# A sparse-attention layer's steps taken in twos, with PSUM banks shared between scores and transposes

## What is computed

```
q = rms_norm(h @ w_in[q]);  kslc, vslc, kwin, vwin from h @ w_in        # 16 heads of 64 in 4 groups
p_c = masked_softmax(q @ k_cmp - slope * dist)                           # compressed branch, 31 blocks
p_s = masked_softmax(q @ kslc  - slope * dist)                           # selected branch
p_w = masked_softmax(q @ kwin  - slope * dist)                           # window branch
o = gate0 * p_c @ v_cmp + gate1 * p_s @ vslc + gate2 * p_w @ vwin
x = x + o @ w_out
```

## Time and profile before

| | us |
|---|---|
| median of 3 runs (2063.76 to 2066.28) | 2065.8 |
| the profiled execution | 2062.16 |
| its span, first to last instruction | 2060.4 |
| PE busy | 2023.5 (98%) |
| DVE busy | 1412.0 (69%) |
| ACT busy | 971.4 (47%) |
| POOL busy | 151.7 (7%) |

### The profile page before, as it was taken

The page is one execution under the profiler, slowest core; times in us unless marked ns, Lnnn a source line. Parts: engine busy times, 40 slices in busy tenths (PEclk is TensorE's granted clock), DMA queues, the critical chain, the costliest instruction groups (busy, mean ns, idle before and its releaser), DMA issues. The chain is left out here.

```text
span 2060.4 us, 36832 instructions
## 1 busy us (share of the span) xinstructions
PE 2023.5 (98%) x14803; PEld 1756.5 (85%) x14803; DVE 1412.0 (69%) x2743; ACT 971.4 (47%) x1874; POOL 151.7 (7%) x140
## 2 busy tenths in 40 slices
PE   9999999999999999999999999999999999999997
PEld 9997777899988887789999887888888888788986
DVE  5247874988864767578887556766666667586576
ACT  5337982555500266545553004554444453566554
POOL 1113330000000400000000002000000000120000
PEclk9999999999999999999999999999999999999998
DMA  5240001233332221013332321211111110112211
GB/s 188 83 144 22 2 2 62 93 103 104 103 132 82 94 84 62 21 62 113 103 103 93 123 102 51 103 62 62 61 61 61 61 61 20 74 67 103 80 45 42
DMA packets 30664, 159.35 MB, mean 77 GB/s; under 512 B 3392, under 2 KB 3904, under 8 KB 17856
## 3 DMA queue, kind: packets, MB, share of 16 engines
q1 hardware_dynamic: 30240, 157.24, 21.6%
q10 hardware_dynamic: 288, 0.20, 0.0%
HBM read 155.33 MB, written 2.10 MB: 76 GB/s over the span
## 5 line engine op out<-in xcount | busy, mean ns | idle before, releaser
L231 PE MATMUL ps<-late_parts,panel_upper 128*128 128x256 f32 (+1 forms) x1376 | 458.8, 333 | 0.0
L230 PE MATMUL ps<-late_parts,panel_upper 128*128 128x256 f32 (+1 forms) x1260 | 430.3, 342 | 5.4 <-issue 1.8
L232 PE MATMUL ps<-late_parts,panel_parts 128*128 128x256 f32 (+1 forms) x1260 | 424.4, 337 | 0.0
L221 DVE TENSOR_TENSOR panel_parts<-panel_sb,panel_upper 128x512 fp32r<-128x512 f32 (+1 forms) x330 | 321.1, 999 | 14.3 <-ACT panel_upper L734 8.7
L230 PE MATMUL ps<-panel_upper,hT_parts 128*128 128x256 f32 (+2 forms) x964 | 295.1, 306 | 2.2 <-DVE h_lower L919 1.4
L232 PE MATMUL ps<-panel_upper,h_lower 128*128 128x256 f32 (+2 forms) x964 | 283.4, 294 | 0.0
L231 PE MATMUL ps<-panel_parts,hT_parts 128*128 128x256 f32 (+2 forms) x964 | 282.1, 293 | 0.0
L231 PEld LDWEIGHTS ps<-late_parts,panel_upper 128*128 128x128 f32 x1376 | 258.7, 188 | 25.8
L230 PEld LDWEIGHTS ps<-late_parts,panel_upper 128*128 128x128 f32 x1260 | 236.7, 188 | 36.8 <-issue 4.4
L232 PEld LDWEIGHTS ps<-late_parts,panel_parts 128*128 128x128 f32 x1260 | 237.9, 189 | 28.5
L230 PE MATMUL ps<-hT_parts,panel_upper 128*128 128x512 f32 (+1 forms) x492 | 191.8, 390 | 1.7 <-PEq L4268 1.7
(11 more groups left out here) (544 smaller groups left out, 3757.8 us busy)
## 6 DMA issues: line engine op xcount, KB each, us to landing
panel_sb<-ffn_gate_up_w SPq DMA_DIRECT2D x76, 512.0 KB, 4.4
panel_sb<-gdn_w SPq DMA_DIRECT2D x24, 1024.0 KB, 4.8
panel_sb<-ffn_down_w SPq DMA_DIRECT2D x22, 1024.0 KB, 4.9
panel_sb<-nsa_w SPq DMA_DIRECT2D x13, 1024.0 KB, 4.8
panel_sb<-gla_w SPq DMA_DIRECT2D x12, 1024.0 KB, 4.9
panel_sb<-gdn_out_w SPq DMA_DIRECT2D x8, 1024.0 KB, 4.8
panel_sb<-ffn_gate_up_w SPq DMA_DIRECT2D x6, 1024.0 KB, 5.0
panel_sb<-nsa_out_w SPq DMA_DIRECT2D x4, 1024.0 KB, 4.9
```

Of the source, the lines that this page charges most:

```text
L221: return engine.tensor_tensor(out, src, hi.bitcast(F32), ALU.subtract)
L230: mm(out, w_hi, x_hi, start=start, stop=False, skip_group_check=skip_group_check)
L231: mm(out, w_hi, x_lo, start=False, stop=False, skip_group_check=skip_group_check)
L232: return mm(out, w_lo, x_hi, start=False, stop=stop, skip_group_check=skip_group_check)
```

## The change

From step 6 the steps go in twos (a batch is v and v+1 for even v). PE does `scores(v+2)`, `scores(v+3)`, `turn(v)`, `turn(v+1)`, `values(v-1)`, `values(v)`. ACT does `exps(v+2)`, `turned(v)`, `exps(v+3)`, `turned(v+1)`, and after those a pair's `upper_o` and one `upper_out`. DVE does both weightings, then both `biased`, then `head_bias`, `lower_o` and the previous batch's `lower_out`. Scores and transposes share three pairs of PSUM banks; each takes the pair whose last use was earliest, and waits until that use has been read. There are four `prob` buffers instead of three, `POOL_STEPS` is 4, and the fourth compressed group's work moves one step later. Its `cmp_exp` stands ahead of `exps(7)`, and `exps(7)` ahead of the copy of step 5. The diff shows the banks first, then the loops of PE, ACT and DVE.

```diff
-    NB = 3
+    NB = 4
-    POOL_STEPS = 6
-    OUT_PIECE_AT = (8, 9, 10, 13, 15, 18, 19, 20, 23, 24, 25, 28, 33, 34, 35, 38)
+    POOL_STEPS = 4
+    TWOS_FROM = 6
+    OUT_PIECES = 16
...
+    for two in range(TWOS_FROM, STEPS, 2):
+        SHARED += [(SCORE, v) for v in (two + 2, two + 3) if v < STEPS] + [(TURN, two), (TURN, two + 1)]
...
+            banks = min(last_in, key=lambda b: SHARED.index(last_in[b]))
+        BANKS_OF[use], BANKS_BEFORE[use] = banks, last_in[banks]
...
+    def await_banks(pe, use):
+        kind, v = BANKS_BEFORE[use]
+        if kind == SCORE:
+            pe.wait_ge(S("n_biased"), ops_before(v + 1))
+        else:
+            pe.wait_ge(S("n_pT"), v + 1)
...
-            if v == 3:
+            if v == 4:
                 cmp_scores(3)
-            if v == 5:
+        for v in range(TWOS_FROM, STEPS, 2):
+            if v + 2 < STEPS:
+                scores(v + 2)
+                scores(v + 3)
+            turn(v)
+            if v == TWOS_FROM:
                 turn_pc(3)
+            turn(v + 1)
+            values(v - 1)
+            values(v)
...
+            if v == TWOS_FROM - 1:
+                cmp_exp(3)
+                exps(v + 2)
...
+        for v in range(TWOS_FROM, STEPS, 2):
+            for u in (v, v + 1):
+                if u + 2 < STEPS:
+                    exps(u + 2)
+                turned(u)
+                if u == TWOS_FROM:
+                    save_pc(3)
+            for u in (v, v + 1):
+                if u % PAIR_STEPS == 1:
+                    upper_o(u // PAIR_STEPS - 1)
+            if (v - TWOS_FROM) // 2 < OUT_PIECES:
+                upper_out((v - TWOS_FROM) // 2)
...
+        for v in range(TWOS_FROM, STEPS, 2):
+            for u in (v, v + 1):
+                weighted(u)
+            for u in (v + 2, v + 3):
+                if u < STEPS:
+                    biased(u)
+            for pair, ab in BIAS_IN.get(v, []):
+                head_bias(pair, ab)
+            for u in (v, v + 1):
+                if u % PAIR_STEPS == 2:
+                    lower_o(u // PAIR_STEPS - 1)
+            if v > TWOS_FROM:
+                lower_out((v - TWOS_FROM) // 2 - 1)
```

More of the change, by code:

```diff
@@ L285, in build_in @@
     bias_pair0 = take(T)
-    kcmp_st = take(P)
+    kcmp_st = hidden[:, 0, :]
     kc_sum, q_gain = take(1), take(1)
@@ L396, in pair_step @@
         return pair, pieces
+    TURN, SCORE = "turn", "score"
+    SHARED = [(SCORE, 0), (SCORE, 1), (SCORE, 2), (TURN, 0), (SCORE, 3), (TURN, 1)]
+    for v in range(2, TWOS_FROM):
+        SHARED += [(SCORE, v + 2), (TURN, v)]
+    for two in range(TWOS_FROM, STEPS, 2):
+        SHARED += [(SCORE, v) for v in (two + 2, two + 3) if v < STEPS] + [(TURN, two), (TURN, two + 1)]
+    BANKS_OF, BANKS_BEFORE = {}, {}
+    last_in = {0: None, 2: None, 4: None}
+    for n, use in enumerate(SHARED):
+        kind, v = use
+        if v < TWOS_FROM:
+            banks = 4 if kind == TURN else 2 * (v % 2)
+        else:
+            banks = min(last_in, key=lambda b: SHARED.index(last_in[b]))
+        BANKS_OF[use], BANKS_BEFORE[use] = banks, last_in[banks]
+        last_in[banks] = use
+    def await_banks(pe, use):
+        kind, v = BANKS_BEFORE[use]
+        if kind == SCORE:
+            pe.wait_ge(S("n_biased"), ops_before(v + 1))
+        else:
+            pe.wait_ge(S("n_pT"), v + 1)
     def ops_before(v):
@@ L620, in scores @@
             else:
-                pe.wait_ge(S("n_biased"), ops_before(v - 1))
+                await_banks(pe, (SCORE, v))
             for t, br, at, n in pieces:
@@ L626, in scores @@
                         r = head_rows(ab)
-                        last = mm(ps[:, 2 * (v % 2) + ab, at + c:at + end], qT[r, pair, tok(t)], kT[r, br * GROUPS + pair // 2, c:end], start=True, stop=True)
+                        last = mm(ps[:, BANKS_OF[SCORE, v] + ab, at + c:at + end], qT[r, pair, tok(t)], kT[r, br * GROUPS + pair // 2, c:end], start=True, stop=True)
             last.then_inc(S("n_scores"), 1)
@@ L633, in turn @@
             else:
-                pe.wait_ge(S("n_pT"), v)
+                await_banks(pe, (TURN, v))
             for ab in range(2):
@@ L642, in turn @@
                 for tile in range(TT):
-                    last = nc.tensor.transpose(ps[:, 4 + ab, tok(tile)], prob[v % NB][:, ab, tok(tile)], ident[:])
+                    last = nc.tensor.transpose(ps[:, BANKS_OF[TURN, v] + ab, tok(tile)], prob[v % NB][:, ab, tok(tile)], ident[:])
             last.then_inc(S("n_turned"), 1)
@@ L682, in pe_nsa @@
         turn_queries(N_Q[3], 1)
-        for v in range(1, STEPS):
-            if 1 < v < STEPS - 2:
+        for v in range(1, TWOS_FROM):
+            if v > 1:
                 scores(v + 2)
@@ L874, in turned @@
                 act.wait_ge(S("n_valued"), v - 1)
-            nc.scalar.copy(pT[v % 2][:, :, :], ps[:, 4:6, :]).then_inc(S("n_pT"), 1)
+            nc.scalar.copy(pT[v % 2][:, :, :], ps[:, BANKS_OF[TURN, v]:BANKS_OF[TURN, v] + 2, :]).then_inc(S("n_pT"), 1)
         def upper_out(n):
@@ L894, in act_nsa, with copied @@
         exps(2)
-        for v in range(STEPS):
-            if 2 <= v < STEPS - 1:
+        def copied(v):
+            turned(v)
+            if v % PAIR_STEPS == 1 and v > 1:
+                upper_o(v // PAIR_STEPS - 1)
+        for v in range(TWOS_FROM):
+            if v >= 2:
                 exps(v + 1)
+            if v == TWOS_FROM - 1:
+                cmp_exp(3)
+                exps(v + 2)
             if v == 2:
                 save_pc(2)
-            turned(v)
+            copied(v)
             if v == 0:
                 cmp_exp(2)
[L903 to L910, removed]
+        for v in range(TWOS_FROM, STEPS, 2):
[10 more added lines that the diff above has]
+                upper_out((v - TWOS_FROM) // 2)
         upper_o(NPAIR - 1)
@@ L1117, in biased @@
                 for ab in range(2):
-                    nc.vector.tensor_tensor_reduce(out=prob[v % NB][:, ab, at:at + n], in0=ps[:, 2 * (v % 2) + ab, at:at + n], in1=bias_of(pair)[ab][:, T - n:T],
+                    nc.vector.tensor_tensor_reduce(out=prob[v % NB][:, ab, at:at + n], in0=ps[:, BANKS_OF[SCORE, v] + ab, at:at + n], in1=bias_of(pair)[ab][:, T - n:T],
                                                    scale=1.0, scalar=3e38, op0=ALU.add, op1=ALU.min,
@@ L1162, in dve_nsa @@
         save_queries(N_Q[3], 1)
-        for v in range(1, STEPS):
+        for v in range(1, TWOS_FROM):
             if v >= POOL_STEPS:
                 weighted(v)
-            if v + 2 < STEPS:
-                biased(v + 2)
-            if v + 1 < min(POOL_STEPS, STEPS):
+            biased(v + 2)
+            if v + 1 < POOL_STEPS:
                 inverse_sums(v + 1)
-            if v % PAIR_STEPS == 2 and v > 2:
-                lower_o(v // PAIR_STEPS - 1)
             if v == 1:
                 cmp_weights(2)
-            if v == 3:
+            if v == 4:
                 cmp_bias(3)
-            if v == 4:
+            if v == 5:
                 cmp_weights(3)
[L1178 to L1181, removed]
+            if v < 3:
+                head_bias(1, v - 1)
+        BIAS_IN = {}
+        for pair in range(2, NPAIR):
+            free = TWOS_FROM if pair == 2 else max(u for u in range(TWOS_FROM, STEPS, 2) if u < PAIR_STEPS * (pair - 1))
+            for ab in range(2):
+                BIAS_IN.setdefault(free + 2 * ab if pair > 2 else free, []).append((pair, ab))
+        for v in range(TWOS_FROM, STEPS, 2):
[11 more added lines that the diff above has]
+                lower_out((v - TWOS_FROM) // 2 - 1)
         lower_o(NPAIR - 1)
```

## The result

| | before | after |
|---|---|---|
| median, us | 2063.73 (20 runs, 2060.49 to 2066.28) | 2068.78 (20 runs, 2066.09 to 2071.18) |
| the profiled execution, us | 2062.16 | 2067.06 |
| its span, us | 2060.4 | 2065.2 |
| mean granted clock | 0.996 | 0.994 |

The ratio is 1.0024, with an interval of 1.0018 to 1.0030. The changed kernel is slower by 5.05 us by the medians and 4.9 by the profiled executions; the forecast was +8 for the latter, and 2073.8 us for the median. The direction was right and the size too large. Of the 5.0 us between 2073.8 and 2068.78, 3.1 are the profiled execution's own (2070.2 forecast, 2067.06 measured). The other 1.9 are the step from there to the median: 3.6 was added, from three runs of the kernel before; over 20 runs each it is 1.6 before and 1.7 after.

What follows compares the result with a forecast made beforehand. PE was taken to set the pace, ACT close behind. Start 3.8, batches 18 and 28 4.3, end 3.4, less 4.3 idle, gave +7.2; with 0.8 sharing, 2070.2 us profiled, 2073.8 median, range 2065 to 2079.

Steps and rivals of the forecast that it cites:

- The start: Up to values(8): later cmp_scores(3) and cmp_bias delay VectorE's chain, and values(5) waits for save_pc(3); loss 3.8 us.
- Batches 18 and 28: lower_o waits for upper_o on VectorE, so biased and the second transposes come late; 2.15 us each, together 4.3.
- The end: Batch 38, delayed by batch 36 with no scores to cover: ends near 8.5 instead of 5.1, loss 3.4 us.
- Sharing between VectorE and GpSimd: Back-to-back VectorE weightings beside GpSimd's in five delayed batches: 0 to 2.5 us, about 0.55 a time at most; 0.8 taken.
- No order of the steps changes these: PE's group prices, start to next start, were taken as fixed: transposes 1.03, compressed product 1.05, values 1.02, scores 1.08 us.
- its idle time: PE's idle 4.3 us within the 103.4 from scores(12) to the output projection, which the change was to win.
- VectorE's waits of over 3 us for `upper_o`: Sign that the forecast is right: such a wait where turn(9), turn(19) and turn(29) are late.
- The projection: Sign that the forecast is right: the output projection starts 7 to 10 us later than 308.84.
- The one of no change: Rival: start costs less, half the late stands are covered, 2 x 1.1 in batches 18 and 28; +3.3, 2069; chance 0.17.
- ACT did not become the bound: Slower rival: ACT becomes the bound, each batch from 10 on losing 0.4 to a late copy; 2079, chance 0.10.
- The faster rival: Batches run at PE's pace, VectorE's stand at lower_o short; 4.3 idle goes, 1 to 2 stay; -4.5, 2061; chance 0.11.
- My warning of a granted clock under 1.00: Sign that the forecast is wrong: a granted clock under 1.00 in the loop, adding to all; no size given.

Runs made afterwards that it cites:

- e5: The kernel before with only the start of the change (four prob buffers, POOL_STEPS 4, fourth compressed group one step later): 2067.78 us, ratio 1.0017.
- e7: The changed kernel with unread transposes filling PE's gaps ahead of turn(5) and turn(38): 2069.87 us, ratio 1.0031.
- e1: The changed kernel with lower_o of pairs 0, 2, 4 and 6 on VectorE one batch later: 2058.07 us, ratio to before 0.9973.
- e3: The changed kernel with the edits of e1 and e2 together: 2055.56 us, ratio to before 0.9966.
- e8: The same kernel as e3, profiled a second time, nothing changed: 2054.75 us in one run.
- e4: e3, but PE's scores and transposes alternate again within each batch: 2058.08 us, ratio to before 0.9973.
- e2: The changed kernel with cmp_scores(3) one step earlier and cmp_bias(3) ahead of biased(6): 2067.14 us, ratio to before 1.0017.
- e9: The same kernel as e2, profiled a second time, nothing changed: 2066.27 us in one run.

## Why the prediction was right in sign and wrong in size

**The start, +3.8 forecast, 4.2 measured.** Most steps named came: `turn(5)` at 189.45 with the offset, where my terms end the weighting at 189.3, `biased(8)` at 195.5 for my 194.8, `values(5)` at 199.2 for 198.5, `turn(9)` at 206.75 for 206.2. `turn(7)` came at 197.7 for my 196.3, and not behind `biased(8)`: PE itself was late with its groups at the lower clock, and VectorE had stood still for 1.07 us, for `scores(8)`:

```profile
194.98 0.69 DVE L1164 CUSTOM_DVE_ANT_0 arena_sb<-ps,hT_sb 128x512 f32<-128x512 f32 x1 [1.07 <-issue]
```

By e5 some 3.6 of it come with the start's own edits. Part of the agreement is luck: the clock's fall, worth 1.2 us at `values(5)` by e7, was not in the sum, while pairs of `values` and `scores` at steps 6 to 10 were cheaper than I had them.

**Batches 18 and 28, 2 x 2.15 forecast, 2 x 2.63 measured.** The chain was right to 0.3 us: `turn(19)` starts 5.60 into its batch and I had 5.33. `lower_o(2)` is 0.4 later than I had it (1.20 into the batch for 0.76), and some 0.1 is GpSimd at work beside the second weighting; the rest of the chain was a little shorter than its terms. The gap of PE is in two parts, 1.28 for the weighting and 1.18 for `biased`. The other 0.2 of the difference is that batch 18 without the stall is shorter than I assumed: in e1 it has its second transposes at 2.97 (5.89 less 1.02 and 1.90), not 3.17. A stall counts from where the engine would have been, and PE would have been earlier.

**The end, +3.4 forecast, 4.8 measured.** `turn(38)` starts 3.29 into the batch, for my 3.3. Then 0.8 come from the clock (e7), and GpSimd's three weightings take 2.73 us where I had 1.02 and about 1.2:

```profile
307.00 2.73 POOL L1270 TENSOR_SCALAR arena_sb<-arena_sb 128x512 f32<-128x512 f32 x3 [7.49 <-DVE arena_sb L1172]
```

**Sharing between VectorE and GpSimd, 0.8 forecast.** The second weighting takes 0.90 instead of 0.80 for pieces of 128 and 384 columns (above, and the earlier trace rows), and 1.15 for two of 256 at 192.76 where others in the same trace take 0.90. That is 0.10 to 0.25 a time, 0.7 for five: the value taken was right, and its high end of 0.55 a time is not seen. The exclusive hold that the Trainium skill describes (SBUF — State Buffer, "Who interferes with whom") would have kept VectorE waiting at 238.48 until GpSimd's first weighting, begun at 237.87 and some 1.02 long, had ended. This place shows at most 0.10 of that 0.4; whether this weighting is of the kind that takes the hold, no run shows.

**The step that failed: "No order of the steps changes these".** I took the price of each group from a timeline in which each has a neighbour of another kind, and summed 6.26 us a batch. The order does change them. Two groups of one kind in a row take 1.95, 1.92 and 1.90 us, not 2.16, 2.06 and 2.04. In the stretch from `scores(12)` to the projection of e3 there are 14 such pairs of `scores`, 12 of `turn` and 12 of `values` (the others are parted by a wait or a compressed product): 14 x 0.21 + 12 x 0.14 + 12 x 0.14 = 6.3.

| us | forecast | measured |
|---|---|---|
| before, less its idle time | 103.4 - 4.3 | 103.4 - 4.3 |
| cheaper pairs | 0 | -6.3 |
| idle time left in e3 | 0 | +2.9 |
| stalls behind `lower_o` | +7.7 | +9.8 |
| sum, the sharing apart | 106.8 | 105.5 |

The trace has 105.3. The 9.8 is that less the 95.5 of e1 and e3. The 2.9 I read off e3's timeline: 0.3 at the transposes of batches 14, 16, 24, 26, 34 and 36, 0.1 in six others, and 0.36 at the last `values`. In batches 16, 26 and 36 it is a wait for `biased`. By the first three rows e3 should take 95.7, and takes 95.5. So the change has a gain of some 6 us that I did not see, and its stalls cost 2 us and its small waits 3 us more than I gave them.

The whole then reads: the forecast was 8.0 and the span grew by 4.8 (the execution by 4.9). From step 12 on the loop lost 1.9 and not 3.4 + 0.8, which is 2.3 less; the start lost 0.4 more; 0.5 was ahead from before the change and 0.8 is less behind the loop, both of which I had at nothing. Neither is more than the same code varies by between the traces (`cmp_scores(3)`, where it follows `values(2)`, starts between 179.47 in e8 and 180.95 in e4). 8.0 - 2.3 + 0.4 - 0.5 - 0.8 = 4.8.

**The signs and the rivals.** VectorE's waits of over 3 us for `upper_o` came, and the wait of `values(5)`. The projection came 5.6 us later (6.1 with the offset) and not 7 to 10. None of the rivals held as such. The one of no change had 2069, next to the measured 2068.78, but that is luck: by its mechanism the stands of batches 18 and 28 would have been 1.1 us each, and they are 2.63. ACT did not become the bound: with `lower_o` moved (e1) PE runs at its own pace but for the small waits, with ACT's work unchanged. The faster rival said that without VectorE's stand at `lower_o` the loop would win 4.3 less 1 to 2; e1 takes the stand away, and the loop wins 7.9 (103.4 to 95.5), the difference being the pairs' 6.3 less the small waits. My warning of a granted clock under 1.00 came true, worth 1.2 and 0.8 us by e7's landmarks; as the clock's fall differs between executions, these are figures of single traces.

**What stays open.** Why two equal groups in a row cost PE 0.14 to 0.21 us less was not tested. Neither were the shared banks by themselves: the 1.18 us ahead of the second transposes in batches 18 and 28 are a wait for a bank pair, which no transposes had before, so other banks might have saved a part of the stall. The clock's part was never separated by the medians, only in traces. e5's interval of 1.7 to 5.6 us is too wide to split the start further.

## What to carry to other kernels

Read the price of a group on an engine from a place with the neighbours that it will have, not from any undisturbed place: grouping equal work can pay on its own. When work goes in larger batches, look for the one instruction that waits for the end of a batch on another engine and stands at the head of the next (`lower_o` here); moved by one batch it turned a loss of 5 us into a gain of 5, and with the start mended into 10. A gap in PE can cost more than its length, in what runs at half clock behind it; filling one with empty work won nothing here: in its trace the clock fell behind later gaps instead, at two places.

## What the runs showed of the hardware that was not expected

- Groups of small float32 matmuls in pairs of one kind: 1.90 to 1.95 us for two, 1.02 to 1.08 for one between others (e3 and e4, the same work in two orders).
- The granted clock's fall to 0.50 behind a gap in PE is not settled by the gap alone, nor by the program. Behind 3.22 us at the end it fell in the changed kernel, e2 and e9. Behind 2.37 at `turn(5)` it fell in the changed kernel and e5, not in e1. Behind 0.74 and 1.23 it fell in e1, e2 and e7, not in e3, e8 and e9. Behind 1.28 and 1.18 it did not fall in batch 18 of any trace that has them, and in batch 28 it fell in e7 and e9 but not in the changed kernel and e2.
- VectorE's weighting beside one on GpSimd: 0.10 us longer for pieces of 128 and 384 columns, 0.25 for two of 256; GpSimd's three in 2.17 to 2.39 us, 2.73 in the last batch.
